# A one-layer streaming encoder on one core: 192 instead of 160 tokens take the expert mixer's V rows by gather, and GpSimd forms the gate-times-h products

## The reference

```
q = x @ w_query                     # 8 heads, two halves of 128
s = q . sub_keys                    # 128 scores per half
top-16 of each half, 256 sums, top-16 of these -> 16 ids of 16384 experts per head, 128 per token
gates = softmax(best)
h = gelu(x . u_table[ids]);  w = gates * h
out[token] = sum over the token's 128 picks of w * v_table[id]      # rows of 2048
x = LN(alpha * x + out)
```

## Time and profile before

| | us |
|---|---|
| median of 3 runs | 3672.55 (3668.26 to 3704.23) |
| the profiled execution | 3671.08, its span 3669.3 |
| U stage, in Strassen form, ends, V stage starts | about 2540 |
| V stage ends, last norm starts | about 3638 |
| PE busy in 2700 to 3400 | 691.57 of 700 |
| DVE, POOL, ACT busy in 2700 to 3400 | 613.38, 420.18, 194.70 |
| DMA engines busy in 2700 to 3400 | 0.91, at 350 GB/s |

### The profile page before, as it was taken

One profiled execution on the slowest core, in us unless ns is written; L12 is line 12 of the kernel. 1 busy time (PEld: TensorE's weight loads), 2 busy tenths in 40 slices (PEclk: granted clock), 3 DMA queues, 4 the chain that ended last, 5 costly groups with the idle time before them and its releaser, 6 DMA issues.

```text
span 3669.3 us, 62596 instructions
## 1 busy us (share of the span) xinstructions
PE 3529.9 (96%) x25292; PEld 3481.3 (95%) x25292; DVE 2854.3 (78%) x3686; ACT 1196.7 (33%) x1214; POOL 1739.2 (47%) x843
## 2 busy tenths in 40 slices
PE   8999999699799999999999999999999999999996
PEld 7999999699799999999999999999999999999996
DVE  4967769655699987777777777776688888988877
ACT  2332323321422234444444444443222222222223
POOL 3333323143433458878778780001665665665311
PEclk9999999799899999999999999999999999999998
DMA  4222212255424669989889987778799898999862
GB/s 150 73 75 75 80 65 79 75 206 212 147 80 141 199 182 229 231 219 226 231 221 226 230 220 226 229 220 289 272 346 354 346 360 349 342 358 352 348 234 95
DMA packets 466252, 788.23 MB, mean 215 GB/s; under 512 B 78976, under 2 KB 376384, under 8 KB 402384
## 3 DMA queue, kind: packets, MB, share of 16 engines
q1 hardware_dynamic: 337920, 547.99, 45.6%
q0 software_dynamic: 83840, 168.15, 14.7%
q10 hardware_dynamic: 44368, 70.57, 5.2%
HBM read 711.43 MB, written 209.34 MB: 251 GB/s over the span
## 4 chain that ended last, share of the span: by engine, by line
PE 80%; DVE 13%; issue 5%; ACT 1%; POOL 0%; DMA 0%; DVEq 0%; SPq 0%; ACTq 0%; POOLq 0%
PE ps L918 32%; PE ps L697 24%; PE ps L950 20%; DVE yb L1544 2%; DVE y_sp L1872 1%; DVE wl L1855 1%; DVE acc L1849 1%; DVE Wl L1832 1%; PE ps L823 1%; PE ps L773 1%; DVE dist L1432 1%; DVE wt L1826 1%; PE ps L819 1%; DVE qe L1463 1%; PE ps L884 1%
## 5 line engine op out<-in xcount | busy, mean ns | idle before, releaser
L599 POOL TENSOR_TENSOR wl<-wraw,wh 128x2048 fp32r<-128x2048 f32 x88 | 433.5, 4927 | 789.6 <-ACT wh L1029 780.8
L649 POOL DMA_INDIRECT g_scratch<-picks,g_col x384 | 684.1, 1782 | 171.3 <-issue 144.2
L1029 ACT ACTIVATE wh<-wraw 128x2048 fp32r<-128x2048 f32 x216 | 414.0, 1917 | 983.9 <-PE ps L950 744.9
L950 PE MATMUL ps<-Wh,wh 128*128 128x384 f32 x2048 | 688.1, 336 | 17.8 <-DVE Wl L1832 11.2
L950 PE MATMUL ps<-Wl,wh 128*128 128x384 f32 x2048 | 685.9, 335 | 0.0
L950 PE MATMUL ps<-Wh,wl 128*128 128x384 f32 x2048 | 685.8, 335 | 0.0
L918 PE MATMUL ps<-xh,wl 128*128 128x272 f32 x1792 | 518.5, 289 | 0.0
L918 PE MATMUL ps<-xl,wh 128*128 128x272 f32 x1792 | 515.5, 288 | 0.0
L918 PE MATMUL ps<-xh,wh 128*128 128x272 f32 x1792 | 515.2, 287 | 0.3 <-DVE wl L1758 0.3
L697 PE MATMUL ps<-xh,wh 128*128 128x272 f32 x2304 | 488.8, 294 | 27.0 <-POOL xl L621 13.5
L697 PE MATMUL ps<-xh,wl 128*128 128x272 f32 x2304 | 480.8, 290 | 0.0
(11 more groups left out here) (301 smaller groups left out, 7162.2 us busy)
## 6 DMA issues: line engine op xcount, KB each, us to landing
wraw<-in_u_t SPq DMA_DIRECT2D x128, 1024.0 KB, 5.2
v_rows<-in_v_t SPq DMA_DIRECT2D x256, 512.0 KB
wraw<-in_v_t SPq DMA_DIRECT2D x128, 1024.0 KB
wraw<-in_w_in SPq DMA_DIRECT2D x40, 1024.0 KB
g_scratch<-zeros ACTq DMA_DIRECT2D x32, 768.0 KB, 4.6
h_scratch<-hb ACTq DMA_DIRECT2D x64, 384.0 KB
gt<-g_scratch SPq DMA_DIRECT2D x64, 384.0 KB, 7.6
hg<-h_scratch SPq DMA_DIRECT2D x64, 384.0 KB, 9.3
```

What stands on the lines that cost most here:

```text
L599: nc.gpsimd.tensor_tensor(wl[:, u], wraw[:, u], f(wh[:, u]), ALU.subtract).then_inc(wlo, 1)
L649: nc.gpsimd.indirect_dma_start(g_elem, bass.IndirectOffsetOnAxis(ap=idx, axis=0), gate, None, compute_op=ALU.add).then_inc(g_put, 16)
L950: ins = mat(out, w[:, u, d * EG + e], m[:, e], start=(begin and e == 0 and w is wh and m is Wh[v]), stop=(end and e == EG - 1 and w is wl))
L1029: go(wh[:, u], wraw[:, u], ACT.Copy).then_inc(whi, 1)
```

## The change

TD falls from 384 to 352, so SD grows to 192: the rest is 64 tokens (XB), folded two ways, with 64 slots; ALL = 192. The slots now lie in tiles 6 to 117 (STEP0 = 6, STEPS = 112), and POOL's code now walks over the tiles with the same table. The products of groups 1 to 15 move from DVE (m = 3..6, two buffers) to POOL (m = 4..7, four buffers `wr`), each waiting for the `w_lows` of four rows before. Those of group 0 stay on DVE. The turn of the rest at the end is split in two halves.

```diff
-TD = 384
+TD = 352
-NB = P // TS
+XB = SD - P
+NB = P // XB
-TOPK_TILES = ((0, P), (P, P), (2 * P, P), (T - P, P), (TD, TS))
+TOPK_TILES = ((0, P), (P, P), (2 * P, P), (T - P, P), (TD, XB))
...
+        wr = [at(f"wr{v}", [P, TD], F32, HG + EG * ROWD + D * 4 + v * ROWD) for v in range(4)]
-        fsum1 = at("fsum1", [P, T], F32, M0)
+        fsum1 = at("fsum1", [P, T], F32, X0)
...
+        STEP0, STEPS = 6, (NG - 1) * EG - 8
+
+        def slots_at(n):
+            i = n - STEP0
+            return range(i * ALL // STEPS, (i + 1) * ALL // STEPS) if 0 <= i < STEPS else ()
...
+            def w_products(g, q):
+
+                pool.wait_ge(g_in[q], g * 16 + 16)
+                pool.wait_ge(h_in[q], g * 16 + 16)
+                for e in (2 * q, 2 * q + 1):
+                    pool.wait_ge(w_s, g * EG + max(0, e - 3))
+                    nc.gpsimd.tensor_tensor(wr[e % 4][:], hg[:, e], gt[:, e], ALU.mult).then_inc(wp_s, 1)
+
             for s in range(HB):
                 h_gather(s)
-            for s in range(ALL):
-                v_gather(s)
-                if s + HB < ALL:
-                    h_gather(s + HB)
+            for n in range((NG - 1) * EG):
+                if n % EG >= 4:
+                    w_products(n // EG + 1, n % EG - 4)
+                for s in slots_at(n):
+                    v_gather(s)
+                    if s + HB < ALL:
+                        h_gather(s + HB)
...
-            for k in range(KT):
-                ins = mat(ps[:, TURN, k * TS:(k + 1) * TS], y_x[:, k * P:(k + 1) * P], fold[:], start=True, stop=True)
-            ins.then_inc(y_turn, 1)
-            v_group(NG - 1, 1)
+            for j in range(NB):
+                if j:
+                    pe.wait_ge(y_sp_u, 5)
+                for k in range(HK):
+                    ins = mat(ps[:, TURN, k * XB:(k + 1) * XB], y_x[:, (j * HK + k) * P:(j * HK + k + 1) * P], fold[:],
+                              start=True, stop=True)
+                ins.then_inc(y_turn, 1)
+                v_tile(NG - 1, 1, 0, j)
+            v_tiles(NG - 1, 1, 1)
...
-                    go(Wh[v][:, e], wt[e % 2][:], ACT.Copy).then_inc(wh_s, 1)
+                    go(Wh[v][:, e], wr[e % 4][:], ACT.Copy).then_inc(wh_s, 1)
...
-            def w_products(g, es):
-
-                v_.wait_ge(g_in[es[0] // 2], g * 16 + 16)
-                v_.wait_ge(h_in[es[0] // 2], g * 16 + 16)
-                for e in es:
-                    v_.wait_ge(w_s, g * EG + es[0])
-                    C.inc(tt_(wt[e % 2][:], hg[:, e], gt[:, e], ALU.mult), wp_s)
...
-                    C.inc(tt_(Wl[v][:, e], wt[e % 2][:], f(Wh[v][:, e]), ALU.subtract), w_s)
+                    C.inc(tt_(Wl[v][:, e], wr[e % 4][:], f(Wh[v][:, e]), ALU.subtract), w_s)
...
-            STEP0, STEPS = EG, (NG - 1) * EG - EG - 2
...
-                if 3 <= m < 7:
-                    w_products(g + 1, [2 * (m - 3), 2 * (m - 3) + 1])
```

More of the change, by code:

```diff
@@ L277, in program @@
         y_x = at("y_x", [P, D], F32, G0 + 3 * D * 4)
-        HG = G0 + 4 * D * 4
-        assert M0 + 4 * ROW <= HG and HG + EG * ROWD <= M0 + 4 * ROW + 2 * HK * TH * 4
+        HG = M0 + 4 * ROW
+        assert G0 + 4 * D * 4 <= HG and HG + EG * ROWD <= M0 + 4 * ROW + 2 * HK * TH * 4
         y_sp = at("y_sp", [P, D], F32, HG + EG * ROWD)
-        assert HG + EG * ROWD + D * 4 <= M1
+        wr = [at(f"wr{v}", [P, TD], F32, HG + EG * ROWD + D * 4 + v * ROWD) for v in range(4)]
+        assert HG + (EG + 4) * ROWD + D * 4 <= M1
         acc = at("acc", [P, KT, T], F32, M1)
@@ L286, in program @@
         assert (EG + 2) * ROWD <= 15520
-        fsum1 = at("fsum1", [P, T], F32, M0)
-        fsum2 = at("fsum2", [P, T], F32, M0 + ROW)
-        fsq = [at(f"fsq{u}", [P, T], F32, M0 + (2 + u) * ROW) for u in range(2)]
+        fsum1 = at("fsum1", [P, T], F32, X0)
+        fsum2 = at("fsum2", [P, T], F32, X0 + ROW)
+        fsq = [at(f"fsq{u}", [P, T], F32, X0 + (2 + u) * ROW) for u in range(2)]
         XT = HK * TH * 4
@@ L1235, in score_evict @@
                 go(sc[:, slot, 0:4].rearrange("p q k -> p (q k)"), ps[:, 4 + 2 * (slot % 2), :], ACT.Copy)
-                go(sc[0:TS, slot, 4], ps[0:TS, 5 + 2 * (slot % 2), 0:P], ACT.Copy).then_inc(s_out, 1)
+                go(sc[0:XB, slot, 4], ps[0:XB, 5 + 2 * (slot % 2), 0:P], ACT.Copy).then_inc(s_out, 1)
             for n in range(SC):
@@ L1721, in _ @@
             C.done(ts_(s_h[:], s_w[:], float(SD), s_tok[:], ALU.mult, ALU.add), dve)
-            C.done(ts_(s_h[:], s_h[:], float(TS), None, ALU.add), dve)
+            C.done(ts_(s_h[:], s_h[:], float(XB), None, ALU.add), dve)
             C.done(cp(s_hid[:], s_h[:]), dve)
             def rest(a):
-                return picks[0:TS, a, REST].rearrange("p h k -> p (h k)")
+                return picks[0:XB, a, REST].rearrange("p h k -> p (h k)")
             C.done(stt_(r_f[:], rest(1), float(P), rest(2), ALU.mult, ALU.add), dve)
             cp(r_ids[:], r_f[:])
-            C.done(ts_(r_f[:], r_f[:], float(SD), s_tok[0:TS], ALU.mult, ALU.add), dve)
+            C.done(ts_(r_f[:], r_f[:], float(SD), s_tok[0:XB], ALU.mult, ALU.add), dve)
             C.done(cp(r_hid[:], r_f[:]), dve)
-            C.done(tt_(fold[:], ident[:, 0:TS], ident[:, TS:2 * TS], ALU.add), dve)
-            for b in range(2, NB):
-                ins = tt_(fold[:], fold[:], ident[:, b * TS:(b + 1) * TS], ALU.add)
-                C.done(ins, ids_s if b == NB - 1 else dve)
+            C.done(tt_(fold[:], ident[:, 0:XB], ident[:, XB:2 * XB], ALU.add), ids_s)
             def flat(a):
@@ L1893, in _ @@
             v_lo_first(1)
-            STEP0, STEPS = EG, (NG - 1) * EG - EG - 2
-            def slots_at(n):
-                i = n - STEP0
-                return range(i * ALL // STEPS, (i + 1) * ALL // STEPS) if 0 <= i < STEPS else ()
             assert SLOTS in slots_at((NG - 3) * EG) or SLOTS < slots_at((NG - 3) * EG)[0]
@@ L1933, in _ @@
                 add_y((NG - 1) * EG + k // 2, k % 2)
+                if k == 3:
+                    add_rest(1, dve)
                 if k % 2 and k < KT - 4:
```

46 lines of the change are left out of this document (25 added, 21 removed).

## The result

The changed kernel takes 3738.58 us (median of 5 runs, 3735.03 to 3749.30) against 3672.55: 1.0168 times as long, 95% interval 1.0127 to 1.0209. It is slower by 66 us. The forecast was 3708, in a range of 3640 to 3765, with slower by over 1% as the likeliest sign (0.43, against 0.42 for within 1%). Sign and range held, the sign by odds that were nearly even, so there is luck in it; the 36 us forecast were little more than half of the loss, so a term was too small, and which one is the question of what follows. Some executions of the kernel before took 3692 to 3704 us instead of 3664 to 3676, at a mean granted clock of 0.973 to 0.975 instead of 0.976 to 0.979, and as the ratios use all executions, those of after and of e1 to e8 lie 0.1 to 0.3% under the quotient of the medians.

What follows compares the result with a forecast made beforehand. PE was taken as the bound, with DVE, POOL and DMA not far behind. 3671 + 25 (tiles 6 to 98) - 2 (99 to 117) - 10 (without slots) + 20 (start) + 3 (clock) = 3707, put at 3708 us; range 3640 to 3765.

Steps and rivals of the forecast that it cites:

- PE's term: V stage matmuls: 32 columns fewer save 0.65 us per tile, 8.30 to 7.65; alone, 83 us over 128 tiles.
- The start: V stage start: group 1's products stand behind 32 h_gathers; PE stands 20 us (10 to 26), plus 3 for the clock.
- Tiles 6 to 98: V stage tiles with slots and h_gathers: 8.70 us per tile against 8.43, +25 us.
- How they combine: Tiles 6 to 98: DVE 8.0, DMA 8.0, POOL up to 9.0, each waiting for the others, give 8.70 (7.65 to 9.4).
- wait for gathers that stand behind products: POOL's in-order queue, m = 6 and 7: products hold back the gather behind them, 0 to 3 us twice a group.
- Tiles 99 to 117: V stage tiles with slots but without h_gathers: 8.30 us per tile, -2 us.
- The tiles without slots: The 16 V stage tiles without slots: PE's 0.65 us saved in each, -10 us.
- The port: POOL's products block DVE instructions with two SBUF inputs: 0.7 us each taken, up to 0.93; DVE needs 8.0 per tile.
- DMA: V stage traffic of 3.19 MB per tile: 8.0 us per tile, showing as 365 to 375 GB/s.
- A: Rival, heavier jam: POOL does not get between DVE's instructions; 9.2 us per tile, +86, 3758 us; chance 0.20.
- B: Rival: slots keep the present pace, products slip into add_y, DMA limits at 8.3 us per tile; about 3675; chance 0.21.
- C: Rival, faster: products fall on add_y, DVE needs 7.4, PE sets the pace; 8.0 us per tile, 3637; chance 0.17.

Runs made afterwards that it cites:

- e1: Changed kernel, but POOL forms group 1's first six products among its 32 first h_gathers, not behind all of them: 3738.65 us, 1.0173.
- e8: e2 with the slots from tile 8 on and in 110 tiles, as in the kernel before: 3686.99 us, 1.0020.
- e3: Kernel before (384 columns, 160 slots), but POOL forms the products into four buffers in the changed kernel's order: 3715.48 us, 1.0111.
- e4: Changed kernel without the 160 h_gathers behind the first 32: 3711.29 us, 1.0101.
- e6: Changed kernel, but from the fourth V gather on each brings half a row: 3743.05 us, 1.0164.
- e7: e1 with the slots from tile 8 on and in 110 tiles, as in the kernel before: 3744.49 us, 1.0165.
- e2: Changed kernel with the products back on DVE at m = 3 to 6, two buffers, none on POOL: 3689.86 us, 1.0036.
- e12: Kernel before with its 160 slots dealt out by weight over a group, fewest at m = 4 to 6: 3662.47 us, 0.9973.
- e5: e2, but from the fourth V gather on each brings half a row: 3678.92 us, 0.9993.
- e14: Changed kernel with its 192 slots dealt out by weight over a group, fewest at m = 4 to 7, from tile 8 on: 3776.61 us, 1.0284.
- e15: e11 with a fourth buffer for V rows, in the room of the wr buffers: 3655.18 us, 0.9962.
- e11: e8 with its 192 slots dealt out by weight over a group, fewest at m = 4 to 6: 3702.54 us, 1.0076.

## Why the prediction was right in sign and too small

**PE's term: right.** 158.7 ns per matmul, 159 to 160 forecast.

**The start: right in size.** V tile 7 is written 18.7 us late; 20 + 3 less four for narrower tiles was forecast. The 32 h_gathers end at 2596.2 (2599 forecast), the products follow at once. In e3, e4 and e6 PE shows the one wait for `wl` that was named, of 17.4, 19.5 and 19.6 us. In the profiled execution of after it doesn't: PE crept through tiles 3 and 4 instead, at nearly the same bill (below). But the meaning of the term was wrong. e1, e7 and e8 show that it isn't part of a sum: taken away, it is given back. And one wait was missed: slot 0 now stood in tile 6, ahead of its 32 elements: it is the +10.0 us of e2 at V tile 8, and in after it is hidden under the other wait.

**Tiles 6 to 98: the step that failed.** T = 8.70 was forecast, +25 us; it is some 9.0, +49 (from +18.7 to +67.9). DVE's need was right, 629/78 = 8.07 per tile (8.0 forecast); POOL's, 589/78 = 7.5, lies between its bounds of 5.5 and 9.0. Wrong was "How they combine": I set means over all tiles side by side and took a value between DVE's 8.0 and POOL's 9.0. `w_lows`, POOL's two products per tile and the port time that they cost DVE all fall on m = 4 to 7. At m = 4 to 6 DVE is busy for 10.0, 10.1 and 9.8 us, nearly without a wait, and the tiles take just that; with buffers one tile deep the tiles at m = 1 and 2, which take 8.4 and 7.9, can't make up for it. e12 shows the same in the kernel before, where it was hardly felt: with slots taken off m = 4 to 6 these tiles take 8.6, 8.3 and 8.3, before 8.9, 8.8 and 8.8. But that is not the whole 0.3 us per tile. By the forecast's 0.7 us per product and the prices of e5 DVE has 1.03 + 2.28 + 1.03 + 4.03 + 2 x 0.7 = 9.8 us at m = 4 to 7, and (4 x 9.8 + 4 x 7.65)/8 = 8.7: the forecast's 8.70 again, and e4's. What lies above it is in the main POOL's instructions, 0.34 us per tile by e4. Their place is m = 0, the tile that rose most (from 7.5 to 8.9): DVE waits 1.9 us for gathers there, and in e4, without the h_gathers, it takes 7.7. The wait for gathers that stand behind products was named ("0 to 3 us twice a group"); it comes once a group. A last part is the clock, which was priced at the start alone: the 35 us above, by which PE's tile at m = 0 is 9.2 instead of 7.7. No run separates it from the rest, and e14 shows that slots merely moved away from m = 4 to 7 win nothing in this kernel.

**Tiles 99 to 117: wrong.** -2 forecast, +4 measured (+67.9 to +71.6 at V tile 121). The h_gathers are over there, but a tile still takes 8.9 us (1074 matmuls in 200 us) and a v_gather instruction still 1.93 us, as in the tiles up to 98. *The tiles without slots: right.* Six of the 16 lie in the start's term and win four of its us; from V tile 121 to the end it goes from +71.6 to +65.2, -6 as forecast.

**The port: right.** Products have a minimum of 0.92, a mean of 1.19 and go to 3.0, slots to 4.7. 0.7 us per product were taken. 132 slots longer by 0.25 and 76 `w_lows` longer by 0.32 are 57 us for the 78 products of the window, 0.73 each; on the two `w_lows` of the rows above it is 3.14 - 0.95 = 2.2 for two. `wl` was named among those that would stretch and doesn't in after, where from 2620 to 3600 only 4 of 109 met a product; in e3, where 22 did, 9 stretched, up to 3.1 us. The Trainium skill ("SBUF — State Buffer", section "Who interferes with whom") calls the shared port pair an exclusive lock; the rows agree: POOL's 1.84 us lie in full on DVE's two. POOL's indirect DMAs wait for DVE in a like way: in e2 the 77 that started beside a `wl` ended 0.82 us after it (median; shortest 0.81) and took 2.43 us in the mean, the 50 beside an `add_y`, one of whose inputs is in PSUM, took 0.94.

**DMA: wrong as a limit here.** 356 GB/s, not 365 to 375; e6 shows that it binds nothing in after. The Trainium skill ("DMA: Bandwidth & Descriptors", section "Where 436 GB/s comes from") puts the HBM side at about 358 GB/s per core; the estimate from that figure, 8.9 us per tile, is near the measured 9.0. The number fits and the cause doesn't: e6 took as long with 254 GB/s, and e15 moved 384 over 700 us.

**The rivals.** A named a jam at 9.2 us per tile and is nearest in size (3758 at 0.20), with a start like the one seen; its mechanism, products that POOL can't get in, is there only in part: ACT waits 84.9 us for products. B's (DMA) and C's are out. That the slots alone would be faster was in none of them, but it was my expectation of e2, and wrong by 66 us: the tables show PE at its own 7.7 us for m = 1 to 4 of e2 and behind DVE's 9.3, 9.2 and 9.0 after that. Of the 83 us that PE's term promised, e2 kept nothing.

## What to carry to other kernels

Add up each engine's work per step of the pipeline, not per tile in the mean: with buffers one step deep the sum of each step's maximum gave e5's 8.5 us, where the means give 7.9. It leaves out waits for gathers and the clock, which come on top, as in after (8.7 by the sum, 9.0 measured). Before work is moved, look which step it lands in, for the engine that gets it and for its neighbours: e12 won 9 us by that, e14 lost 38. A ring of buffers has a pace of its own (its time in use over its depth; e11, e15), and where such a pace rules, what is saved at the start is given back (e1, e7, e8). Taking load off PE pays only as far as the next engine's worst step allows: here 160 slots, spread by weight, gave 9 us for no cost, and 192 needed a fourth row to give 16.

## What was not expected of the hardware

In the profiled execution of after PE's matmuls came singly or in groups of up to six with gaps of up to 1.7 us between 2573 and 2599 (17 gaps, 12.0 us in all, for none of which the profile shows what was waited for); DMA moved almost nothing then, and the granted clock fell from 1.00 to 0.50. Windows of after, 2570 to 2600:

```profile
2570.00:2585.00 15.00, 9.54 (x41) 6.40 (x40) 1.05 (x3) 0.16 (x1) 11.63 (x12) 0.89 0.22 70
2585.00:2600.00 15.00, 8.19 (x19) 4.96 (x20) 4.99 (x3) 2.75 (x3) 12.36 (x12) 0.50 0.07 15
```

e3, e4, e6 and e14, with the same order on POOL, show no such gaps. Counted from `wl` of V tile 1 and against before, V tile 7 is 15.8 to 17.2 us late in them and 18.7 in after. So what it was stays open, and it cost some 3 us at most, since PE would have stood.
